# Layer two of a two-layer mixture-of-experts block: token rows of the first ten experts picked by one-hot products from SBUF, with ten weight homes instead of eleven

## The reference

```python
def grouped_moe(h, router_w, router_bias, w1, w3, w2):
    s = jax.nn.sigmoid((h @ router_w).astype(jnp.float32))
    ...                       # two experts of one group of four per token
    for e in range(N_EXPERTS):                                   # 16
        he = (jax.nn.silu(h @ w1[e]) * (h @ w3[e])) @ w2[e]      # 1024 -> 512 -> 1024
        out = out + combine[:, e:e + 1] * he
    return out
```

## Time and profile before

| | us |
|---|---|
| median of 3 runs | 1107.94 |
| lowest and highest run | 1106.4 and 1112.21 |
| the profiled execution's own time | 1109.42 |
| its span, first to last instruction | 1107.6 |
| PE busy | 931.4 (84%) |
| DVE busy | 458.8 (41%) |
| ACT busy | 246.2 (22%) |
| POOL busy | 193.3 (17%) |

### The profile page before, as it was taken

One profiled execution on the slowest core, in us unless ns is written; L12 is line 12 of the kernel. 1 busy time (PEld: TensorE's weight loads), 2 busy tenths in 40 slices (PEclk: granted clock), 3 DMA queues, 4 the chain that ended last, 5 costly groups with the idle time before them and its releaser, 6 DMA issues.

```text
span 1107.6 us, 23678 instructions
## 1 busy us (share of the span) xinstructions
PE 931.4 (84%) x9036; PEld 547.7 (49%) x9036; DVE 458.8 (41%) x1090; ACT 246.2 (22%) x485; POOL 193.3 (17%) x325
## 2 busy tenths in 40 slices
PE   3999999979987699999778389999888478976795
PEld 2536445545445466768444166543555345543353
DVE  2178336466564433323222387406652622211233
ACT  2100112344322133223122031113531121211121
POOL 4100000110020144444324220000100111110011
PEclk9999999999997699999999889999998699988898
DMA  9997612750003999999999978317802999999994
GB/s 347 390 401 286 255 68 76 265 239 1 1 1 133 376 416 418 417 418 408 398 410 412 382 280 328 109 45 254 343 1 95 371 374 416 415 404 417 412 391 178
DMA packets 53806, 314.32 MB, mean 284 GB/s; under 512 B 6728, under 2 KB 7564, under 8 KB 34768
## 3 DMA queue, kind: packets, MB, share of 16 engines
q1 hardware_dynamic: 42752, 286.93, 64.6%
q0 software_dynamic: 8336, 17.74, 4.4%
q10 hardware_dynamic: 2624, 8.27, 2.0%
HBM read 306.98 MB, written 9.50 MB: 286 GB/s over the span
## 4 chain that ended last, share of the span: by engine, by line
PE 54%; DMA 34%; DVE 5%; issue 3%; DVEq 2%; ACT 1%; SPq 1%; POOL 1%; POOLq 0%; ACTq 0%
PE ps L1965 50%; DMA ring<-in_w 17%; DMA area<-in_w 7%; DMA cst<-in_w 3%; DMA ring<-in_w_in 2%; DMA HT<-in_w 2%; PE ps L2249 2%; DMA expert_rows<-area 1%; DMA XG<-in_w 1%; PE ps L2074 1%; PE ps L2095 1%; DMA area<-expert_rows 1%; DMA area<-h_rows,area 1%; PE ps L2274 0%; PE ps L2285 0%
## 5 line engine op out<-in xcount | busy, mean ns | idle before, releaser
L1965 PE MATMUL ps<-ring,HT 128*128 128x512 f32 (+1 forms) x576 | 254.0, 593 | 2.5 <-issue 2.2
L1965 PE MATMUL ps<-ring,area 128*32 128x256 f32 x3520 | 215.5, 396 | 42.5 <-DMA ring<-in_w 22.6
L1965 PE MATMUL ps<-area 128*32 128x256 f32 (+5 forms) x2024 | 177.8, 397 | 19.3 <-DVE area L1849 10.0
L1965 PEld LDWEIGHTS ps<-ring,area 128*32 128x32 f32 x3520 | 128.1, 114 | 126.1 <-issue 55.5
L1965 PEld LDWEIGHTS ps<-ring,HT 128*128 128x128 f32 x576 | 108.5, 194 | 126.4 <-issue 122.8
L1965 PEld LDWEIGHTS ps<-area 128*32 128x32 f32 (+4 forms) x2024 | 109.0, 147 | 63.2 <-issue 39.1
L1880 DVE STREAM_TRANSPOSE area<-area 128x256 f32<-128x256 f32 x63 | 28.1, 446 | 176.3 <-PE ps L1965 175.4
L1965 PE MATMUL ps<-HT,ring 128*128 128x256 f32 (+1 forms) x320 | 86.6, 428 | 3.0 <-DMA ring<-in_w_in 2.8
L966 POOL DMA_INDIRECT area<-h_rows,area x66 | 69.1, 1047 | 104.9 <-DVEq L1866 43.2
L1965 PEld LDWEIGHTS ps<-HT,ring 128*128 128x128 f32 x320 | 60.7, 193 | 23.6 <-issue 14.3
L1458 DVE SCALAR_TENSOR_TENSOR area<-area,CW 128x512 f32<-128x512 f32 (+1 forms) x120 | 68.8, 615 | 4.5 <-issue 0.5
(11 more groups left out here) (235 smaller groups left out, 866.9 us busy)
## 6 DMA issues: line engine op xcount, KB each, us to landing
ring<-in_w SPq DMA_DIRECT2D x56, 2048.0 KB, 10.8
ring<-in_w_ada SPq DMA_DIRECT2D x24, 2048.0 KB, 17.6
ring<-in_w_in SPq DMA_DIRECT2D x10, 2048.0 KB, 18.7
area<-in_w SPq DMA_DIRECT2D x20, 1024.0 KB, 10.0
HT<-in_w SPq DMA_DIRECT2D x8, 2048.0 KB, 10.6
area<-in_w SPq DMA_DIRECT2D x8, 2048.0 KB, 10.8
late<-in_w SPq DMA_DIRECT2D x8, 1536.0 KB
ring<-in_w_out SPq DMA_DIRECT2D x4, 2048.0 KB, 7.9
```

What stands on the lines that cost most here:

```text
L1965: return t_.matmul(out, lhsT, rhs, start=first, stop=last_)
```

## The change

Only layer two changes.

- `H2` stays in SBUF, so the SPLIT home is given up: ten homes.
- In each step of experts 0 to 9 PE also picks the rows of the next block: eight products behind the up product. These picks bring blocks 1 to 14, that is all other blocks of the ten experts and the first block of expert 10. DVE turns the rows straight from PSUM and makes the one-hot columns of the block after (`choose`: two compares, an add, and a subtraction of 32 from every place).
- POOL gathers only blocks 15 to 23 (and up to three empty ones at the end), from `first + 1` on, through two counts more that DVE makes during routing.
- DVE's copy of gathered rows falls away for the picked blocks.

```diff
+PICKED = 10
...
-            turn += [HT_HOME, AREA_HOME, SPARE_HOME, LATE_HOME, SPLIT_HOME]
+            turn += [HT_HOME, AREA_HOME, SPARE_HOME, LATE_HOME]
         row, last = [], {}
         for n in range(3 * E_N):
-            x = turn[n % HOMES]
+            x = turn[n % len(turn)]
...
+                    def fetch(n, r, column):
+                        if not isinstance(n, int):
+                            hold(pool, xs_rdy[l], n - 1, pool_passed)
+                        g.tensor_copy(gidx[r], TG[:, bass.ds(column, 1)]).then_inc(gidx_set[l], 1)
+                        hold(pool, gidx_set[l], n + 1, pool_passed)
+                        pool.indirect_dma_start(xg[:, r * NW:(r + 1) * NW], None, h2_rows, bass.IndirectOffsetOnAxis(ap=gidx[r], axis=0),
+                                                bounds_check=routed(l) * NG - 1, oob_is_err=False).then_inc(gath[l][r], 16)
+                    column = pool.alloc_register("pool_columns")
+                    pool.reg_add(column, first, 1)
                     for r in range(2):
-                        gather(PEEL + r, r, r)
-                    made = pool.alloc_register("pool_gathers")
-                    pool.reg_mov(made, 2)
-                    with pool.Fori(PEEL // 2 + 1, pairs) as i:
+                        fetch(r, r, pool.snap(column) + r)
+                    with pool.Fori(1, pairs) as i:
+                        pool.reg_add(column, column, 2)
                         for r in range(2):
-                            gather(2 * i + r, r, pool.snap(made) + r)
-                        pool.reg_add(made, made, 2)
+                            fetch(2 * i + r, r, pool.snap(column) + r)
...
+                if l == DEPTH - 1:
+                    v.tensor_copy(nb[:, E_N + 4:E_N + 5], off[:, PICKED:PICKED + 1])
+                    v.tensor_tensor(nb[:, E_N + 6:E_N + 7], off[:, E_N:E_N + 1], off[:, PICKED:PICKED + 1], ALU.subtract)
                 dve.drain()
...
+                def choose():
+                    for k in range(2):
+                        v.tensor_tensor(XO[:, k, 0:nq], rkf[:, k, 0:nq].unsqueeze(2).to_broadcast([P, nq, SLOT]), consts(C_COL, SLOT), ALU.is_equal)
+                    dve.drain()
+                    v.tensor_tensor(XO[:, 0, 0:nq], XO[:, 0, 0:nq], XO[:, 1, 0:nq], ALU.add).then_inc(x0_oh[l], 1)
+                    if l == DEPTH - 1:
+                        v.tensor_scalar(rkf[:, :, 0:nq], rkf[:, :, 0:nq], -float(SLOT), None, ALU.add)
...
-                def step(b):
-                    turn_x(b + 1)
+                def step(b, chosen=False, fetched=None):
+                    if chosen:
+                        dve.drain()
+                    else:
+                        turn_x(b + 1)
                     hold(dve, si_rdy[l], b + 1, dve_passed)
                     v.scalar_tensor_tensor(gg, sg, TW[:, bass.ds(b, 1)], ps[:, B_W13, P:2 * P], ALU.mult, ALU.mult).then_inc(g_rdy[l], 1)
+                    if chosen:
+                        hold(dve, picked, b + 1, dve_passed)
+                        v.transpose(xT, bank(("x0", l))[:, 0:NW]).then_inc(xt_rdy[l], 1)
+                        choose()
                     if not isinstance(b, int) or b:
                         copy_y(b - 1)
                     dve.drain()
                     v.transpose(gT, gg).then_inc(gt_rdy[l], 1)
-                    copy_x(b + 2)
+                    if not chosen:
+                        copy_x(b + 2 if fetched is None else fetched)
...
                     last.then_inc(w13_full[l], 1)
+                    if l == DEPTH - 1 and e < PICKED:
+                        pe.wait_ge(x0_oh[l], b + 2)
+                        for t in range(nq):
+                            for j in range(NG):
+                                last = mm(bank(("x0", l))[SLOT * j:SLOT * (j + 1), 0:NW], XO[:, 0, t], H2[:, t, j * NW:(j + 1) * NW], t == 0, t == nq - 1)
+                        last.then_inc(picked, 1)
```

More of the change, by code:

```diff
@@ L804, in _ @@
                     x, u = EXPERTS[l][n]
-                    first = n < HOMES
+                    first = x not in [home(l, m) for m in range(n)]
                     if n >= RING:
@@ L977, in scatter @@
                                             bounds_check=2 * routed(l) * NG - 1, oob_is_err=False).then_inc(scat[r], 16)
-                for n in range(1, PEEL):
-                    gather(n, n % 2)
-                pairs = pool.value_load(nb[0:1, E_N + 1:E_N + 2], min_val=PEEL, max_val=BMAX // 2 + 2)
                 if l == DEPTH - 1:
+                    first = pool.value_load(nb[0:1, E_N + 4:E_N + 5], min_val=PICKED, max_val=BMAX)
+                    pairs = pool.value_load(nb[0:1, E_N + 5:E_N + 6], min_val=(E_N - PICKED + 2) // 2, max_val=BMAX // 2 + 2)
+                    def fetch(n, r, column):
[7 more added lines that the diff above has]
+                    pool.reg_add(column, first, 1)
                     for r in range(2):
-                        gather(PEEL + r, r, r)
-                    made = pool.alloc_register("pool_gathers")
-                    pool.reg_mov(made, 2)
-                    with pool.Fori(PEEL // 2 + 1, pairs) as i:
+                        fetch(r, r, pool.snap(column) + r)
+                    with pool.Fori(1, pairs) as i:
+                        pool.reg_add(column, column, 2)
                         for r in range(2):
-                            gather(2 * i + r, r, pool.snap(made) + r)
-                        pool.reg_add(made, made, 2)
+                            fetch(2 * i + r, r, pool.snap(column) + r)
                     for i in range(nq):
@@ L995, in _ @@
                     return
+                for n in range(1, PEEL):
+                    gather(n, n % 2)
+                pairs = pool.value_load(nb[0:1, E_N + 1:E_N + 2], min_val=PEEL, max_val=BMAX // 2 + 2)
                 for r in range(2):
@@ L1851, in _ @@
                     last.then_inc(oh_done[l], 1)
+                if l == DEPTH - 1:
+                    v.tensor_scalar(nbi[:, 1:2], nb[:, E_N + 6:E_N + 7], 2.0, None, ALU.add)
+                    dve.drain()
+                    v.tensor_scalar(nb[:, E_N + 5:E_N + 6], nbi[:, 1:2], 1, None, ALU.arith_shift_right)
                 v.tensor_scalar(nb[:, E_N + 3:E_N + 4], nb[:, E_N + 1:E_N + 2], 16.0, -32.0, ALU.mult, ALU.add)
@@ L1855, in _ @@
                 v.tensor_scalar(nb[:, E_N + 2:E_N + 3], nb[:, E_N + 2:E_N + 3], 16.0, 16.0, ALU.mult, ALU.add)
-                for k in range(2):
-                    v.tensor_tensor(XO[:, k, 0:nq], rkf[:, k, 0:nq].unsqueeze(2).to_broadcast([P, nq, SLOT]), consts(C_COL, SLOT), ALU.is_equal)
-                dve.drain()
-                v.tensor_tensor(XO[:, 0, 0:nq], XO[:, 0, 0:nq], XO[:, 1, 0:nq], ALU.add).then_inc(x0_oh[l], 1)
+                def choose():
[3 more added lines that the diff above has]
+                    v.tensor_tensor(XO[:, 0, 0:nq], XO[:, 0, 0:nq], XO[:, 1, 0:nq], ALU.add).then_inc(x0_oh[l], 1)
+                    if l == DEPTH - 1:
+                        v.tensor_scalar(rkf[:, :, 0:nq], rkf[:, :, 0:nq], -float(SLOT), None, ALU.add)
+                choose()
                 key = ("tb", l)
@@ L1884, in copy_x @@
                     if isinstance(n, int):
[L1885 removed]
+                        dve.wait_ge(gath[l][n % 2], 16 * ((n + 1) // 2) if l < DEPTH - 1 else 16 * (n // 2) + 16)
                         at_ = n % 2 * NW
                     else:
[L1888 removed]
+                        hold(dve, gath[l][0], 16 * ((n + 2 * l) // 2), dve_passed)
                         hold(dve, gath[l][1], 16 * ((n + 1) // 2), dve_passed)
@@ L1926, in _ @@
                 dve.drain().then_inc(xt_rdy[l], 1)
-                copy_x(1)
+                if l == DEPTH - 1:
+                    dve.drain()
+                    choose()
+                    dve.drain()
+                    chosen = dve.value_load(nb[0:1, E_N + 4:E_N + 5], min_val=PICKED, max_val=BMAX)
+                    others = dve.value_load(nb[0:1, E_N + 6:E_N + 7], min_val=E_N - PICKED, max_val=BMAX)
+                else:
+                    copy_x(1)
                 for b in range(PEEL):
-                    step(b)
+                    step(b, l == DEPTH - 1)
                 copied = dve.alloc_register(f"dve_blocks_{l}")
                 dve.reg_mov(copied, PEEL - 1)
-                with dve.Fori(PEEL, blocks) as b:
-                    step(b)
-                    dve.reg_add(copied, copied, 1)
+                if l == DEPTH - 1:
+                    with dve.Fori(PEEL, chosen) as b:
+                        step(b, True)
+                        dve.reg_add(copied, copied, 1)
+                    copy_x(0)
+                    with dve.Fori(0, others) as n:
+                        step(dve.snap(copied) + 1, fetched=n + 1)
+                        dve.reg_add(copied, copied, 1)
+                else:
+                    with dve.Fori(PEEL, blocks) as b:
+                        step(b)
```

(1 more changed line is left out.)

7 lines of the change are left out of this document (4 added, 3 removed).

## The result

| | before | after |
|---|---|---|
| median, 20 runs each | 1112.19 us | 1118.62 us |
| lowest and highest run | 1106.40 and 1118.77 | 1112.01 and 1128.39 |
| the profiled execution's own time | 1109.42 | 1119.61 |
| its span | 1107.6 | 1117.8 |

After over before is 1.0065, with a 95% interval from 1.0047 to 1.0084. The change costs about 7 us, where 1.8 us less had been forecast. The loss is small, but its interval lies clear of 1.

What follows compares the result with a forecast made beforehand. The weight stream was taken to bound until expert 12's third unit landed at 1044.0 us, then PE. Terms -3.1, +0.5 and +0.8 gave -1.8 us: 1107.6 for the profiled execution, 1106.1 as a median, range 1102.5 to 1112.5.

Steps and rivals of the forecast that it cites:

- what the clock gave back: PE before 1044 us: 12.6 us lost to the lower clock; with less idling a third, 4.2 us, would return.
- The slack: PE's five DMA waits before 1044.0 us, 13.5 us together, were taken as spendable, making PE ready at 1030.5.
- The pauses: PE's waits put down to issue, 23.2 us, were left as they are.
- Gathers: Weight stream: 14 blocks no longer gathered before 1044 us, 0.22 us each, would save 3.1 us.
- Unit 10: Weight stream at expert 1's start: this unit issued 2.3 us later, costing the stream 0.5 us.
- Ten homes: Weight refills wait for homes: unit 16 late by 1.6 us, unit 19 by 2.7; 0.8 us cost to the stream.
- PE's work: Steps of the ten experts: eight pick matmuls, 0.97 us a block; 14 picks and later start add 13.9 us.
- DVE's additions: DVE's steps: net 0.43 us more each, covered by the wait for the down product, 56.4 us over 24 blocks.
- PE becomes the bound: Rival at PE's arrival at 1044 us: picks at 1.40 us each, no clock gain, 1114.3 us; chance 0.14.
- its marker: Sign for PE as the bound: a chain of waits that is PE's from before 1000 us.
- The homes starve the stream: Rival in the weight stream: delays of 2.3, 1.6 and 2.7 us all show, less 3.1: 1111.4 us; chance 0.12.
- The gathers cost the stream more: Rival in the weight stream: without gathers a unit lands each 5.0 us instead of 5.24, 1101.4 us; chance 0.09.

Runs made afterwards that it cites:

- the picks' work alone: Eight unused pick-shaped matmuls added to each step of experts 0 to 9 of the kernel before, gathers and eleven homes kept: 1116.01 us, 1.0063.
- the two kernels without jumps: Kernels before and after, each without the never-run second step copy of nine one-block experts in PE's program: 1109.90 us, 0.9992 and 1107.05 us, 0.9972.
- ten homes alone: Kernel before with SPLIT given up in layer two, gathers and all else kept: 1113.18 us, 1.0038.
- thin loads: Kernels before and after, layer two's loads cut to one row per partition from a home's second unit on: 1092.97 us, 0.9838 and 1101.87 us, 0.9918.
- the kernel with aligned code: Kernel after with each layer-two expert's PE code, from expert 1, moved to an aligned address by padding that is jumped over: 1203.63 us, 1.0842.

## Why the prediction was wrong, point by point

**The step that failed** is "It waited for DMA five times, 13.5 us together ... So it would have been ready at 1044.0 - 13.5 = 1030.5. That is the slack that the change can spend", with "The waits put down to issue, 23.2 us ..., I leave as they are". Redo PE's sum with measured terms: 1030.5, plus 0.8 for the later start, plus 14 x 1.00 for the picks, minus what the clock gave back. The latter was 7.0 us and not 4.2: by the prediction's durations the records would take 110.5 + 14.0 = 124.5 us at the full clock, and took 130.1, so 5.6 us are lost where it was 12.6. That gives 1038.3. PE came at 1052.35. The missing 14 us are the 13.5 us of "slack" and the 0.4 by which idle time grew. So the step had two faults: the slack was too large, and the pauses put down to issue did not stay as they were.

*The slack.* The profile puts an idle time down to one cause alone. The five waits for weights stand at experts 11 and 12. Three of them before; the longer two are right behind the jumps of experts 10 and 11:

```profile
1016.99 3.64 PE L1965 MATMUL ps<-ring,area 128*32 128x256 f32 x32 [5.26 <-DMA ring<-in_w]
1022.30 1.93 PE L1965 MATMUL ps<-ring,area 128*32 128x256 f32 x32 [1.67 <-DMA ring<-in_w]
1032.01 1.08 PE L1965 MATMUL ps<-ring,area 128*32 128x256 f32 x6 [4.84 <-DMA ring<-in_w]
```

The same steps after, where no weight is late:

```profile
1031.36 2.35 PE L2016 MATMUL ps<-ring,area 128*32 128x256 f32 x37 [1.85 <-issue]
1035.39 1.92 PE L2016 MATMUL ps<-ring,area 128*32 128x256 f32 x27 [1.68 <-issue]
1043.18 1.93 PE L2016 MATMUL ps<-HT,area 128*32 128x256 f32 x32 [2.92 <-issue]
1047.89 1.70 PE L2016 MATMUL ps<-area 128*32 128x256 f32 x20 [1.06 <-issue]
```

From expert 11's first product to expert 12's second block PE was idle for 14.0 us before, 13.5 of it for weights, and for 8.4 us after. These two experts have no picks in either kernel. So 5.6 us of the waits could be spent, and 8.4 us lay over pauses that stay. With the picks' work alone it is 8.8 us there.

*The pauses.* Before expert 11 PE was idle for 22.7 us, and after the change for 28.7, 6.0 more, where the prediction left "issue" alone. Most of it is at experts 9 and 10: 3.2 and 2.8 us before, 4.8 and 5.3 after. With the picks' work alone the sum is 26.0 us, 3.3 more. The added matmuls make the code longer (25 packets for 22) and move all that follows; which of the two makes the new pauses is not told apart. The two faults together, 7.9 and 6.0 us, are the missing 14, and idle time as a whole came out as before, 36.7 and 37.1 us. That the two sums agree is chance.

**The stream.** Gathers: 3.1 us forecast, 2.8 read between the two kernels without jumps, with the doubt named there. Unit 10: forecast 2.3 us later, was 4.8, and the sag was 91 GB/s at a share of 0.35 against 229 and 0.64; the 2 us more are the pause of 1.93 us between the turned rows and expert 1's first product. Ten homes: units 16 and 19 were forecast 1.6 and 2.7 us late, and were 4.3 and 5.0 (922.60 and 938.24 against 918.35 and 933.22), for the same reason. These didn't reach the end, as unit 38 landed 159.5 us into the stretch. By the Trainium skill, "DMA: Bandwidth & Descriptors", section "Anatomy of one DMA", the prediction had an estimate by which a refill late by under 3.2 us does not show. That section of the Trainium skill has its 2.0 us from transfers that POOL issues, and SP issues these weights. No run here tests the estimate by itself. With ten homes alone units 10 and 16 went out 2.9 us later in the stretch than before (889.63 and 919.83, with its first up product at 882.97), unit 40 was 4.8 us later, and the kernel 0.38% slower; but units 13 and 15 were 3.6 us later, beyond the 3.2 of the estimate.

**PE's work.** 0.97 us a pick forecast, 1.00 measured. Granted clock up from 0.90 to 0.95: right in sign, more than forecast, but not for the reason given. The prediction had PE idle less, and its idle time stayed the same. DVE's additions were covered as forecast: in the stretch it has next to no part in the chain (0.46 us at 889.84), and its wait for the down product went from 56.4 us to 45.1. Nothing was late on ACT or POOL.

**The rivals.** "PE becomes the bound" had a chance of 0.14, a time of 1114.3 us, and the right sign. Its mechanism was half right: the chain is PE's from the start, as its marker said. Its price was wrong. It asked for 1.34 us or more a pick, and the picks cost 1.00. The rest came from the pauses, of which it, too, took no account. That its 1114.3 us lie nearer to the result is luck. "The homes starve the stream" holds for the homes alone (1113.2 us against 1109.6); in the whole change PE is later still and covers it. "The gathers cost the stream more" got its 5.05 us a unit only where the jumps are gone.

**What stays open.** Which code addresses make pauses long, and where a hint would help, if anywhere. What the first pause of a pair is: it goes with the jump, but no packet stands in it or right before it, so that it is a fetch is not shown. Whether the change would be a gain with a general cure for the jumps: the pair without jumps points that way within its noise, and no general version was built.

## What to carry to other kernels

Time that an engine waited for a late transfer is slack only if nothing else was being waited for at the same time. Before spending it, look at the same place in an iteration without the late transfer: if "issue" pauses of a few microseconds stand there, expect them under the covered ones as well. Here 5.6 of 13.5 us were left. A cheap test is to add the planned work as idle instructions, with nothing else changed; here it gives 1.0063, where the whole change has 1.0065.

An "issue" gap in the middle of an operation is a reason to look at the instruction queue: in the pairs above such gaps ended 2.2 to 2.6 us after a packet of code had begun. The shorter gaps of 0.8 to 0.9 us, and the 1.8 to 1.9 us right behind a jump, often have no packet beside them. In this kernel, whose engines branch on counts, the rarely taken copy of a long unrolled body cost time even when it was skipped.

## What the runs showed of the hardware

- Behind a jump over a long body, in the first four of the pairs above, PE stood still for 1.77 to 1.94 us with the full stream and 1.76 to 1.85 with thin loads, and a second time 14 to 37 matmul records later, for 1.7 to 3.5 us with the full stream and 0.9 to 2.2 with thin loads.
- Instruction packets are 16 KB, 22 of them in 159.7 us, 0.9% of the DMA engines' time. That is almost nothing for the stream, but not for PE: without the skipped copies and their jumps there were eight packets fewer in the kernel after, and 27.2 of the 39.0 us of "issue" were gone.
- Each of these second pauses ended 2.2 to 2.6 us after a packet had begun, with the full stream or thin loads. With the full stream the packet began 0.8 to 1.4 us later.
- In the kernel with aligned code PE went on 3.5 us after a packet had begun, once while the weight queue was busy for only 2.6% of the time.
- The same executed matmuls at aligned addresses, with jumps over the filling, took 7.7% longer than in the kernel after (1.0842 over 1.0065).
- The sum of PE's gaps alone does not say what clock TensorE is granted. With 36.7 and 37.1 us of idle time in the stretch it was 0.90 before and 0.95 after. With 25.8 us (thin loads, after) it was 0.98, and 0.80 with 100.6 us (aligned code).
